# Refill order of a ring of weight slots, x at the head of the weight queue, and an attention norm matmul moved ahead of its unit's scores

## What is computed

```python
mod = silu(cond) @ w_ada + b_ada                      # 1024 -> 6 x 1024, per layer
sh1, sc1, g1, sh2, sc2, g2 = split(mod, 6)
h = rms_norm(x, norm1) * (1 + sc1) + sh1
qa, ka, va, hy, qr, kr, vr, gr = split(h @ w_in)
ya = rms_norm(diff_attention(qa, k_all, v_all), subln) # two softmax maps a head, 4 heads
yb = hyena(hy)                                         # short conv, then a long one by DFT
yc = rms_norm(retention(qr, kr, vr)) * silu(gr)
ga, gb, gc = split(sigmoid(h @ w_gate + b_gate), 3)
merged = ga*(ya @ w_a) + gb*(yb @ w_b) + gc*(yc @ w_c)
x = x + g1 * (merged @ w_out)
x = x + g2 * moe(rms_norm(x, norm2) * (1 + sc2) + sh2) # 16 experts, top 2 of one group
```

## Time and profile before

| what | value |
| --- | --- |
| median of 3 runs | 1329.48 us (1329.24 to 1331.26) |
| the profiled execution | 1329.32 us |
| its span, first to last instruction | 1327.5 us |
| busy, share of span | PE 94%, PEld 71%, DVE 28%, ACT 17%, POOL 1% |
| mean granted TensorE clock | 0.973 |
| DMA | 358.47 MB, mean 270 GB/s |

### The profile page before, as it was taken

The page is one execution under the profiler, slowest core; times in us unless marked ns, Lnnn a source line. Parts: engine busy times, 40 slices in busy tenths (PEclk is TensorE's granted clock), DMA queues, the critical chain, the costliest instruction groups (busy, mean ns, idle before and its releaser), DMA issues.

```text
span 1327.5 us, 18353 instructions
## 1 busy us (share of the span) xinstructions
PE 1246.0 (94%) x7708; PEld 941.3 (71%) x7708; DVE 368.2 (28%) x915; ACT 221.6 (17%) x435; POOL 13.5 (1%) x29
## 2 busy tenths in 40 slices
PE   4989999999989999999979999999999899999994
PEld 3768888878876666666547888887887676666652
DVE  1441153133235111121243223413233511111113
ACT  2141012231021100111024101323101110000111
POOL 1000000000000000000000000000000000000000
PEclk9999999999989999999989999999999799999997
DMA  9598333334677999999937833342344499999990
GB/s 390 192 382 349 132 136 135 127 113 155 240 277 299 419 420 421 421 420 418 413 131 280 355 127 135 115 150 102 133 153 162 163 422 419 421 420 421 421 384 34
DMA packets 49996, 358.47 MB, mean 270 GB/s; under 512 B 5680, under 2 KB 5696, under 8 KB 7152
## 3 DMA queue, kind: packets, MB, share of 16 engines
q1 hardware_dynamic: 47808, 348.15, 65.7%
q0 software_dynamic: 2096, 9.03, 1.8%
HBM read 354.53 MB, written 2.62 MB: 269 GB/s over the span
## 4 chain that ended last, share of the span: by engine, by line
PE 88%; DVE 4%; DMA 4%; ACT 2%; issue 1%; SPq 0%; DVEq 0%; POOL 0%; ACTq 0%
PE bank L641 24%; PE bank L921 15%; PE bank L957 9%; PE bank L829 6%; PE bank L904 5%; PE bank L850 4%; PE bank L998 4%; PE bank L652 3%; PE bank L636 3%; PE bank L567 3%; DMA ring<-in_experts 2%; DMA ring<-in_weights 2%; PE bank L625 1%; PE bank L936 1%; ACT gates L1425 1%
## 5 line engine op out<-in xcount | busy, mean ns | idle before, releaser
L641 PE MATMUL bank<-h,ring 128*128 128x256 f32 x1472 | 328.6, 382 | 0.0
L641 PEld LDWEIGHTS bank<-h,ring 128*128 128x128 f32 x1472 | 278.5, 191 | 44.1 <-issue 7.2
L921 PE MATMUL bank<-ring,gates 128*64 128x256 f32 x2048 | 225.2, 380 | 4.4 <-ACT gates L1425 3.7
L921 PEld LDWEIGHTS bank<-ring,gates 128*64 128x64 f32 x2048 | 150.7, 137 | 76.5 <-issue 6.4
L957 PE MATMUL bank<-ring,gates 128*64 128x512 f32 x512 | 113.4, 595 | 5.4 <-ACTq L1428 5.4
L957 PEld LDWEIGHTS bank<-ring,gates 128*64 128x64 f32 x512 | 41.4, 137 | 67.0 <-issue 67.0
L904 PE MATMUL bank<-uc,gates 128*128 128x128 f32 x576 | 69.5, 280 | 0.0
L904 PEld LDWEIGHTS bank<-uc,gates 128*128 128x128 f32 x576 | 68.2, 198 | 0.0
L1516 DVE SCALAR_TENSOR_TENSOR gates<-gates,bank 128x512 f32<-128x512 f32 (+1 forms) x18 | 11.8, 658 | 181.0 <-issue 135.7
L998 PEld LDWEIGHTS bank<-gates,uc 128*128 128x128 f32 x256 | 47.3, 190 | 18.8 <-issue 13.0
L998 PE MATMUL bank<-gates,uc 128*128 128x256 f32 x256 | 59.5, 386 | 0.0
(11 more groups left out here) (235 smaller groups left out, 1064.9 us busy)
## 6 DMA issues: line engine op xcount, KB each, us to landing
ring<-in_experts SPq DMA_DIRECT2D x204, 1024.0 KB, 11.0
ring<-in_weights SPq DMA_DIRECT2D x128, 1024.0 KB, 5.5
par<-in_params POOLq DMA_DIRECT2D x2, 749.5 KB, 12.4
cst<-in_consts POOLq DMA_DIRECT2D x1, 1473.0 KB, 16.0
x<-in_x_in POOLq DMA_DIRECT2D x1, 1024.0 KB, 9.8
sc<-in_s_cache POOLq DMA_DIRECT2D x2, 512.0 KB, 5.9
y_out<-h POOLq DMA_DIRECT2D x2, 512.0 KB, 2.9
kc<-in_k_cache POOLq DMA_DIRECT2D x2, 256.0 KB, 4.0
```

The costliest lines, as they stand in the source:

```text
L641: last = pe.matmul(bank[b][:, c * TOK:(c + 1) * TOK], w[:, k, c * P:(c + 1) * P], h[:, k, :], start=(k == 0), stop=(k == KT - 1))
L921: last = pe.matmul(bank[b][64 * j:64 * j + 64, half * 256:half * 256 + 256], hgat[:, k, 64 * j:64 * j + 64], w[j][:, k, :], start=(k == 0) ...
```

## The change

Three things are done.

1. `DONE` is the order in which pieces are given back, which differs from PLAN in the opening alone (ada(0, 1) ahead of units 0, 1 and 2). `ring_table` computes from it the slot (`SLOT`) and the fill count (`FILL`) of each piece. Piece n goes into the slot of the piece that is given back as number n - 8. ada(0, 1) now raises `s_weights_used` itself, by 4, at its own end; `s_ada_second` is gone. In layer 0, ada item 2 follows unit 4 in place of unit 3, and item 3 uses bank 5 in place of 4.
2. x and shd are the first two transfers on SP's queue, ahead of all weights; they are gone from POOL's. POOL waits for the landing of the four pieces of ada(0, 0) before it issues the large constants and the parameters behind them.
3. `o_norm(2)` stands ahead of `att_scores`, `att_turn` and `att_out` of unit 25. On DVE `o_scale` is cut in two: `o_mean` (reading bank 7, freeing it) is called for j = 2 ahead of `soft_max(5)`; `o_scale` keeps the rest.

```diff
-ADA_AFTER = {(0, 3): 2, (0, 5): 3, (0, 7): 4, (1, 1): 2, (1, 3): 3, (1, 5): 4}
+ADA_AFTER = {(0, 4): 2, (0, 5): 3, (0, 7): 4, (1, 1): 2, (1, 3): 3, (1, 5): 4}
+OPENING = [("ada", 0, 0), ("proj", 0, 0), ("proj", 0, 1), ("proj", 0, 2), ("ada", 0, 1)]
+OPENING_DONE = [("ada", 0, 0), ("ada", 0, 1), ("proj", 0, 0), ("proj", 0, 1), ("proj", 0, 2)]
+def ada_bank(layer, u):
+    return {(0, 5): 5, (0, 7): 7}.get((layer, u), 4)
...
-END = {item: sum(PLAN_PIECES[kind] for kind, _, _ in PLAN[:n + 1]) for n, item in enumerate(PLAN)}
+DONE = OPENING_DONE + PLAN[len(OPENING):]
+END = {item: sum(PLAN_PIECES[kind] for kind, _, _ in DONE[:n + 1]) for n, item in enumerate(DONE)}
+def ring_table():
+    pieces = [(item, c) for item in PLAN for c in range(PLAN_PIECES[item[0]])]
+    done = [(item, c) for item in DONE for c in range(PLAN_PIECES[item[0]])]
+    slot, count, filled = [], [], [0] * SLOTS
+    for n, piece in enumerate(pieces):
+        at = n if n < SLOTS else slot[pieces.index(done[n - SLOTS])]
+        filled[at] += 1
+        slot.append(at)
+        count.append(filled[at])
+    return slot, count
+SLOT, FILL = ring_table()
...
         def _(sp):
+            sp.dma_start(x[:, :, :], x_in).then_inc(s_x_in, 16)
+            sp.dma_start(shd[:, :], shared).then_inc(s_shared_in, 16)
...
-                    sp.dma_start(ring[:, n % SLOTS, :], weights[dense, :, :]).then_inc(
-                        s_weights_in[n % SLOTS], 16)
+                    sp.dma_start(ring[:, SLOT[n], :], weights[dense, :, :]).then_inc(
+                        s_weights_in[SLOT[n]], 16)
...
         def _(pool):
-            pool.dma_start(shd[:, :], shared).then_inc(s_shared_in, 16)
             pool.memset(condT[:, :, :], 0.0).then_inc(s_cond_zero, 1)
             pool.memset(ones[:, :], 1.0).then_inc(s_ones_set, 1)
-            pool.dma_start(x[:, :, :], x_in).then_inc(s_x_in, 16)
             pool.dma_start(cst[:, 0:P], consts[:, 0:P]).then_inc(s_ident_in, 16)
             pool.dma_start(modp[:, :, :], mod_params).then_inc(s_mod_params_in, 16)
+            for slot in range(ADA_PIECES):
+                pool.wait_ge(s_weights_in[slot], 16)
             pool.dma_start(cst[:, P:N_CST], consts[:, P:N_CST]).then_inc(s_consts_in, 16)
...
-                pe.wait_ge(s_weights_in[n % SLOTS], 16 * (n // SLOTS + 1))
-                return ring[:, n % SLOTS, :].rearrange("p (k n) -> p k n", n=width)
+                pe.wait_ge(s_weights_in[SLOT[n]], 16 * FILL[n])
+                return ring[:, SLOT[n], :].rearrange("p (k n) -> p k n", n=width)
...
-                if (layer, q) == (0, 1):
-                    last.then_inc(s_ada_second, 1)
-                else:
-                    last.then_inc(s_weights_used, 4)
+                last.then_inc(s_weights_used, 4)
...
-                    last.then_inc(s_weights_used, 5 if u == 2 else 1)
+                    last.then_inc(s_weights_used, 1)
...
-                        ada(layer, ADA_AFTER[layer, u], 7 if u == 7 else 4)
+                        ada(layer, ADA_AFTER[layer, u], ada_bank(layer, u))
...
+                    if u == 25:
+                        o_norm(layer, 2)
                     if u in SCORES_AT:
                         att_scores(layer, SCORES_AT.index(u))
                     if u - 1 in SCORES_AT:
                         att_turn(layer, SCORES_AT.index(u - 1))
                     if u - 2 in SCORES_AT:
                         att_out(layer, SCORES_AT.index(u - 2))
-                    if u == 25:
-                        o_norm(layer, 2)
...
-                if (layer, q) == (0, 1):
-                    sc_e.wait_ge(s_ada_second, 1)
-                else:
-                    sc_e.wait_ge(s_weights_used, END["ada", layer, q])
+                sc_e.wait_ge(s_weights_used, END["ada", layer, q])
...
-                def o_scale(j, b=6):
+                def o_mean(j):
                     dve.wait_ge(s_o_norm_sum, 4 * layer + j + 1)
                     link(ts(rinv[:, :], bank[7][:, :], 1.0 / DV_A, ALU.mult, EPS, ALU.add))
                     dve.sem_inc(s_bank_free[7], 1)
                     dve.sem_inc(s_o_mean, 1)
+                def o_scale(j):
                     dve.wait_ge(s_o_root, 4 * layer + j + 1)
                     link(dve.reciprocal(rinv[:, :], tmp[:, :]))
...
                 def yc(g):
+                    o_mean(g)
                     o_scale(g)
...
                 for i in range(8):
+                    if i == 5:
+                        o_mean(2)
                     soft_max(i)
                     soft_mix(i)
                     if i == 5:
                         ya(0)
+                o_mean(3)
                 ya(1)
```

More of the change, by code:

```diff
@@ L79, in weight_plan @@
         if layer == 0:
-            plan += [("ada", 0, 0), ("proj", 0, 0), ("proj", 0, 1), ("proj", 0, 2), ("ada", 0, 1)]
+            plan += OPENING
         for u in range(0 if layer else 3, U_MERGE):
@@ L302, in trunk_program @@
         s_mod_ready = sem("mod_ready")
-        s_ada_second = sem("ada_second")
         s_ident_in = sem("ident_in")
@@ L486, in _ @@
                             sp.wait_ge(s_weights_used, n - SLOTS + 1)
-                            sp.dma_start(ring[:, n % SLOTS, :], experts[layer, bass.ds(e, 1), part, :, :]
+                            sp.dma_start(ring[:, SLOT[n], :], experts[layer, bass.ds(e, 1), part, :, :]
                                          .rearrange("a p c -> (a p) c")).then_inc(
-                                             s_weights_in[n % SLOTS], 16)
+                                             s_weights_in[SLOT[n]], 16)
                             n += 1
@@ L494, in _ @@
                         sp.wait_ge(s_weights_used, n - SLOTS + 1)
-                        sp.dma_start(ring[:, n % SLOTS, :], experts[layer, e_, part]).then_inc(
-                            s_weights_in[n % SLOTS], 16)
+                        sp.dma_start(ring[:, SLOT[n], :], experts[layer, e_, part]).then_inc(
+                            s_weights_in[SLOT[n]], 16)
                         n += 1
@@ L499, in _ @@
                     sp.wait_ge(s_weights_used, n - SLOTS + 1)
-                    sp.dma_start(ring[:, n % SLOTS, :], experts[layer, bass.ds(e, 1), part, :, :]
-                                 .rearrange("a p c -> (a p) c")).then_inc(s_weights_in[n % SLOTS], 16)
+                    sp.dma_start(ring[:, SLOT[n], :], experts[layer, bass.ds(e, 1), part, :, :]
+                                 .rearrange("a p c -> (a p) c")).then_inc(s_weights_in[SLOT[n]], 16)
                     n += 1
@@ L1057, in _ @@
                     if (layer, u) in ADA_AFTER:
-                        ada(layer, ADA_AFTER[layer, u], 7 if u == 7 else 4)
+                        ada(layer, ADA_AFTER[layer, u], ada_bank(layer, u))
                     if (layer, u - 1) in ADA_AFTER:
-                        ada_turn(layer, ADA_AFTER[layer, u - 1], 7 if u == 8 else 4)
+                        ada_turn(layer, ADA_AFTER[layer, u - 1], ada_bank(layer, u - 1))
                     if u == 7:
@@ L1278, in _ @@
                     if (layer, u) in ADA_AFTER:
-                        mod_rows(layer, ADA_AFTER[layer, u], 4)
+                        mod_rows(layer, ADA_AFTER[layer, u], ada_bank(layer, u))
                     if u == 2:
@@ L1678, in _ @@
                     if (layer, u - 1) in ADA_AFTER:
-                        mod_add(layer, ADA_AFTER[layer, u - 1], 4)
+                        mod_add(layer, ADA_AFTER[layer, u - 1], ada_bank(layer, u - 1))
                     if u == 2:
@@ L1685, in _ @@
                     if (layer, u) in ADA_AFTER:
-                        mod_add(layer, ADA_AFTER[layer, u], 7 if u == 7 else 4)
+                        mod_add(layer, ADA_AFTER[layer, u], ada_bank(layer, u))
                 cosw, sinw = wide(C("cos"), 4), wide(C("sin"), 4)
```

## The result

The changed kernel takes 1318.97 us (median of 4 runs, 1317.01 to 1321.46). The kernel before takes 1330.37 us beside it (4 runs, 1329.24 to 1332.91). The ratio is 0.9913, with an interval of 0.989 to 0.9936: faster by 11.4 us between the medians, where 15.0 were forecast. The median lies 0.5 us above the forecast range. The profiled execution took 1318.54 us with a span of 1316.7, so the span is 10.8 us shorter.

What follows compares the result with a forecast made beforehand. TensorE (PE) was taken to bound the kernel for 88%, transfers 4%. Gains of 5.8 (refill order), 2.0 (x first) and 7.2 (norm, 3.6 a layer) sum to 15.0: 1329.3 - 15.0 = 1314.3 us; range 1311.8 to 1318.5, 8 in 10.

Steps and rivals of the forecast that it cites:

- The stall did not move to ada(0, 3): Rival at ada(0, 3): its last piece lands up to 4.06 us late, clock behind it; 1320.1 us, chance 0.05.
- The wait of 0.85 us forecast at `att_out`: Attention, each layer: PE reaches `att_out(4)` at 275.5 and waits 0.85 us for the scaling, replacing the wait removed.
- The chain through ACT and DVE: Attention norm: table load ends at 271.5, root 272.2, reciprocal 275.6, scaling 276.35; unit 27 starts at 276.8.
- The rival in which the switch of tables costs more: Attention norm, before the root: the switch costs 1.28 us more, delaying unit 27 in each layer; 1316.9 us, chance 0.12.
- landed at 28.7, 1.9 us ahead of PE: Opening: parameters issued on POOL's queue at 16.3 land at 28.7, before PE reaches filter step 0 at 30.6.
- the 2 that the sum took: Opening, POOL's queue: constants and parameters begin to move some 2 us after their issue at 16.3.
- the opening gives nothing: Rival: late parameters mean PE is at filter step 0 no earlier than before; 1316.3 us, chance 0.12.
- at 32.7 or later: Sign of the rival in which the opening gives nothing: the time by which layer 0's parameters land.
- The halved clock is possible there: Opening, ada(0, 0): after 3.4 us of idle PE it was taken at 5.35 us, ending at 21.8.
- the bytes allow ada(0, 1) at 40.5: Opening: its last piece lands at 40.4 with full queues, so ada(0, 1) starts at 40.7, a 2.0 us gain.
- POOL's queue is served beside SP's: Opening: the two queues share transfers; the slower rival, POOL's not served beside SP's, gives 1327.1 or 1339.1 us, chance 0.04.
- Every wait behind these places is on an event that moves along with PE: Rest of the kernel, behind the three parts: nothing takes gains back, so the full 15.0 us reaches the end time.

Runs made afterwards that it cites:

- the repeat: The changed kernel measured once more, on one chip with the change without x first, against the kernel before (1330.1 us): 1318.36 us, ratio 0.9908.
- the filling matmuls: Changed kernel with constants and parameters on SP's queue, plus matmuls with unread output in PE's idle stretches of the opening: 1316.45 us, 0.9894 against the kernel before.

## Why the prediction was nearly right, and where it failed

**Part 1, right.** 5.8 forecast; 5.87 between the profiles and 5.6 alone. The idle time and the lower clock behind it both went. The stall did not move to ada(0, 3): no wait of ada on a piece is left behind the opening.

**Part 3, right in its mechanism, 0.5 us a layer too high.** 3.6 forecast, 3.12 measured. The wait of 0.85 us forecast at `att_out` was 0.93. The chain through ACT and DVE ran as worked out: from `o_norm`'s start the scaling ends after 271.14 + 0.76 - 261.04 = 10.86 us, against 276.35 - 265.58 = 10.77. The size was off in two small terms behind it. From the scaling's end to `att_out`'s start there are 0.20 us (272.10 - 271.90), which I had left out. And its two groups of matmuls take 0.68 us and not 0.44, since I had taken them as they ran when nothing was waited for. The rest is rounding at each step. The rival in which the switch of tables costs more did not happen: the load at 265.80 takes 1.28 us and the root starts at 267.10, 0.02 behind it. The part stays at 3.12 a layer, and not the 2.2 that the Trainium skill's figure for a switch (page ScalarE: Activation LUTs, section What ACT_TABLE_LOAD costs) would have made.

**Part 2, failed: 2.0 forecast, 0 measured.** The step that failed is "landed at 28.7, 1.9 us ahead of PE". They landed at 34.03. Of the issue on POOL and the landing the page and the timeline of the changed kernel show:

```profile
17.95 0.54 POOL L538 DMA_DIRECT2D cst<-in_consts  x1 [15.40 <-DMA ring<-in_weights]
...
18.47 0.54 POOL L543 DMA_DIRECT2D par<-in_params  x1
```

```profile
par<-in_params POOLq DMA_DIRECT2D x1, 749.5 KB, 15.6
```

Where those 15.6 us went, the packets of the two queues show: the first line is from 18 to 21.6 us, the other two from 21.6 to 28.5 (packets, MB, share; q1 is SP's queue, q0 POOL's).

```profile
q1 hardware_dynamic: 215, 1.52, 100.7%
...
q0 software_dynamic: 171, 1.67, 57.6%
q1 hardware_dynamic: 172, 1.26, 43.6%
```

Up to 21.6 nothing of POOL's queue moved. So the 5.3 us are four terms:

- The issue came at 17.95 instead of 16.3: the fourth piece landed 1.1 us later than forecast, and POOL woke 0.6 us behind it. 1.65 us.
- The constants began to move 3.7 us after their issue, and not the 2 that the sum took. No row showed those 2. 1.7 us.
- They took 6.9 us to their landing at 28.5, and not 6.1. POOL's queue had the half share that was forecast, or a little more; beside it went more of SP's pieces and the first of the parameters. 0.8 us.
- The parameters landed 5.5 us after them instead of 4.3. 1.2 us.

In the four other executions with POOL's wait the issue came at 16.85 to 17.85 and the first packet 3.7 to 3.8 us behind it. The constants landed 10.3 to 11.6 us after their issue, instead of 2 + 6.1 = 8.1. The fourth term is in none of the four: 4.3 us, as forecast. The parameters landed there at 32.1 to 33.1. So the part of the miss that is always there, 2.2 to 3.5 us, is what the constants need from issue to landing, above all the late start of POOL's queue. On SP's queue, in order, the same 2.28 MB landed at 21.67 and held up no piece that the chain waited for.

That is the rival called "the opening gives nothing", at 1316.3 us, for which the prediction named "one late start of POOL's queue". Its mark, "at 32.7 or later", was met in two of the five executions and missed by 0.2 to 0.6 us in the others. It had 0.12 and should have had more than half.

The rest of part 2 held. x lands at 5.6 and ada(0, 0) starts at 16.5 to 17.6. The halved clock is possible there (5.38 us), the bytes allow ada(0, 1) at 40.5, and POOL's queue is served beside SP's. (The idle time ahead of ada(0, 0) is 16.5 - 7.4 - 5.49 = 3.6 us by the prediction's own places, and not 3.4; nothing hangs on it.) But its gain was also priced as if every microsecond of the opening stood in the end time. With the parameters early, x first gave 0.3 us alone. On top of parts 1 and 3 it showed once (1316.66 against 1318.97, from two sets of runs, so weakly). Which of the two is the rule isn't settled here. "Every wait behind these places is on an event that moves along with PE" held for the stage that I had suspected, layer 1's experts.

In numbers: 15.0 forecast, minus 2.0 for part 2, minus 2 x 0.48 for part 3, plus 0.07 for part 1, is 12.1. The first comparison gave 11.4, the repeat 11.7. The interval of either is some 2 to 3 us wide on each side, so the rest is not resolved, and that it comes this near is no proof of the 0.5 us a layer. The 1.35 us lost in the profiled opening are the parameters again: they landed at 34.03, where filter step 0 had run at 32.81 before.

## What to carry to other kernels

When a load is held back behind an event, cost it from the event to its landing, and look in the trace for when its queue's first packet moves: here that was 3.7 us after the issue. Where the order of need is known, put it into the full queue at its place rather than on a second queue behind a wait. A lead of 2 us at one place is not yet 2 us at the end. Follow it through the places behind, in more than one execution: here single profiles of one stage differed by 2.5 us, and an explanation from one of them did not hold over seventeen. A norm whose sum is ready early should also have its root issued early: between the same two places, moving the matmul alone gave 3.1 us a layer, moving root and scaling with it 4.3.

## What the runs showed of the hardware

- The clock in the opening differs between executions of nearly the same work. Behind an idle time of 3.41 us ada(0, 0) took 3.66 us in one execution, behind one of 3.43 it took 4.94 in another (the kernel with the root moved). The first half of unit 0 starts behind an idle time of 2.52 us in most of them. Its 16 matmuls took 3.69, 5.26, 6.45 and 6.65 us in four profiles.
- An idle time of 1.4 us can have the lower level behind it, or not. With the loads on SP's queue and the filling matmuls, ada(0, 1) took 5.35 us after one of 1.35, up to 40.56; the granted clock was 0.59 from 40.56 to 43 and 1.00 before. In the kernel before, ada(0, 0) took 3.66 us after one of 1.45.
- POOL's queue beside a full queue of SP: the first packet moved 3.7 to 3.8 us after the issue. The 1473 KB landed 10.3 to 11.6 us after it, and the 749.5 KB behind them 4.3 to 5.5 us later (five profiles). Alone on its queue, the load of the next layer's parameters took 5.0 us in the kernel before.
- A table load on ACT in the path of the norm took 1.28 us, and the next instruction began 0.01 to 0.02 us behind it, in both places shown (265.80 and 267.10; 260.42 and 261.71).
- Layer 1's experts, with transfers at 420 GB/s throughout, lose some 1.1 us to them: 227.0 us with whole pieces and 225.9 with half ones, from the first matmul on an expert's weights to the start of the last item.
